# Order of the expert weight requests in the later pairs, and the place of VectorE's update of H

## The reference

```
for i in range(DEPTH):                       # 4 layers
    y = mixer_i(h)
    h = layer_norm(DN_ALPHA * h + y, ...)
    m = grouped_moe(h, ...)                  # for each of 16 experts e, with its gates:
                                             #   hidden = silu(t @ w1[e]) * (t @ w3[e]);  out += gate * (hidden @ w2[e])
    h = layer_norm(DN_ALPHA * h + m, ...)
```

## Time and profile before

| | us |
|---|---|
| median of three runs (lowest, highest) | 1929.92 (1926.3, 1935.45) |
| time of the profiled execution | 1932.07 |
| its span, first to last instruction | 1930.3 |
| TensorE busy | 1756.9 (91%) |
| VectorE busy | 683.1 (35%) |
| ScalarE busy | 456.9 (24%) |
| GpSimd busy | 149.1 (8%) |
| mean granted TensorE clock, as a share | 0.957 |
| DMA, mean over the span | 261 GB/s, 504.47 MB |

### The profile page before, as it was taken

One profiled execution on the slowest core, in us unless ns is written; L12 is line 12 of the kernel. 1 busy time (PEld: TensorE's weight loads), 2 busy tenths in 40 slices (PEclk: granted clock), 3 DMA queues, 4 the chain that ended last, 5 costly groups with the idle time before them and its releaser, 6 DMA issues. The chain is left out here.

```text
span 1930.3 us, 24276 instructions
## 1 busy us (share of the span) xinstructions
PE 1756.9 (91%) x8962; PEld 894.9 (46%) x8963; DVE 683.1 (35%) x1391; ACT 456.9 (24%) x894; POOL 149.1 (8%) x113
## 2 busy tenths in 40 slices
PE   8998979989897899899899988897989988899987
PEld 7867643333574443333244544332348757433332
DVE  3444462222425542222312226221243444532223
ACT  2664211111214111111111101111123834111111
POOL 1024100000300100000020100000030131100000
PEclk9999989999998899999999998898999999899999
DMA  9521168999932557679964236699993320579995
GB/s 336 188 95 46 50 273 359 428 428 423 338 131 87 196 231 311 243 304 429 406 248 168 109 158 283 261 410 395 427 357 131 131 88 2 196 299 427 428 428 204
DMA packets 84085, 504.47 MB, mean 261 GB/s; under 512 B 8259, under 2 KB 16500, under 8 KB 59132
## 3 DMA queue, kind: packets, MB, share of 16 engines
q1 hardware_dynamic: 72944, 488.65, 63.2%
q10 hardware_dynamic: 11020, 14.07, 2.2%
HBM read 501.64 MB, written 1.06 MB: 260 GB/s over the span
## 5 line engine op out<-in xcount | busy, mean ns | idle before, releaser
L1989 PE MATMUL bank<-ring,work 128*64 128x512 f32 x2176 | 476.9, 595 | 15.1 <-issue 10.4
L1989 PEld LDWEIGHTS bank<-ring,work 128*64 128x64 f32 x2176 | 156.4, 138 | 327.7 <-issue 319.0
L1507 DVE TENSOR_TENSOR work<-bank,work 64x512 f32<-64x512 f32 x64 | 67.9, 1062 | 539.2 <-ACT work L952 539.1
L1653 PE MATMUL bank<-HT,ring 128*128 128x256 f32 x1024 | 231.8, 387 | 0.0
L1653 PEld LDWEIGHTS bank<-HT,ring 128*128 128x128 f32 x1024 | 198.6, 194 | 37.2 <-issue 10.2
L1661 PE MATMUL bank<-ring,HT 128*128 128x512 f32 x448 | 197.4, 600 | 0.0
L2007 PE MATMUL bank<-w_slot,work 128*64 128x512 f32 x544 | 132.5, 632 | 18.6 <-DMA w_slot<-in_e_w 17.0
L952 ACT ACTIVATE work<-bank 64x512 f32<-64x512 f32 x64 | 37.7, 589 | 425.7 <-PE bank L1989 425.7
L1661 PEld LDWEIGHTS bank<-ring,HT 128*128 128x128 f32 x448 | 85.2, 193 | 103.6 <-issue 103.6
L2033 PE MATMUL bank<-work 128*128 128x512 f32 x256 | 121.4, 618 | 11.1 <-ACT work L977 6.0
L2007 PE MATMUL bank<-work 128*64 128x512 f32 x544 | 125.6, 604 | 5.6 <-DMA work<-in_e_w 4.0
(11 more groups left out here) (294 smaller groups left out, 1583.4 us busy)
## 6 DMA issues: line engine op xcount, KB each, us to landing
ring<-in_e_w SPq DMA_DIRECT2D x128, 2048.0 KB, 14.3
w_slot<-in_e_w SPq DMA_DIRECT2D x32, 2048.0 KB, 14.5
work<-in_e_w SPq DMA_DIRECT2D x32, 2048.0 KB, 16.5
ring<-in_a_w_in SPq DMA_DIRECT2D x15, 2048.0 KB, 20.1
ring<-in_c_w_in SPq DMA_DIRECT2D x8, 2048.0 KB, 23.8
ring<-in_b_w_in SPq DMA_DIRECT2D x6, 2048.0 KB, 24.6
ring<-in_a_w_out SPq DMA_DIRECT2D x4, 2048.0 KB, 8.5
ring<-in_c_w_out SPq DMA_DIRECT2D x4, 2048.0 KB, 7.7
```

The costliest lines, as they stand in the source:

```text
L1507: v.tensor_tensor(by_m(h_[j]), bank[b][CAP:, :], sil[j][CAP:, :], ALU.mult).then_inc(drained[b], 1)
L1653: ins = mm(dst[:, 0:SEQ], wt[:, k, n * P:(n + 1) * P], HT[:, k, :], start=k == 0, stop=k == KC - 1)
L1989: ins = mm(bank[b][lo:lo + CAP, :], x[:, k, :], wt[:, k, :], start=k == 0, stop=k == KC - 1, skip_group_check=True)
```

## The change

Two things are changed. First, `refill` is no longer a hardware loop but is written out seven times, and for p = 3 to 6 it asks in another order: behind step 1 the tiles q = 2, 3 of pair p + 1 as before, then, behind steps 3 and 4, the two down weights of pair p + 1, and only then the tiles q = 0, 1 of pair p + 2. Since step 4 is then past, these two are asked for right behind the down weight of half 1. For p = 0 to 2 the order stays. Second, VectorE's update of H becomes a function and is called in pair 0 behind the product of half 0, and with it the check for an extra pass of expert 0.

```diff
-                    def refill(p, d, more):
+                    def refill(p, d, more, down_first):
                         freed(i, p, 1)
                         for q in (2, 3):
                             load_up((n + 4 * (d + 1) + q) % SLOTS, i, p + 1, q)
-                        if more:
-                            freed(i, p, 2)
-                            for q in (0, 1):
-                                load_up((n + 4 * (d + 2) + q) % SLOTS, i, p + 2, q)
-                        for j in range(2):
-                            freed(i, p, 3 + j)
-                            load_down(i, p + 1, j)
-
-                    with sp.Fori(0, 2) as it:
-                        for d in range(3):
-                            refill(it * 3 + d, d, True)
-                    refill(6, 6, False)
+                        for part in (1, 0) if down_first else (0, 1):
+                            if part:
+                                for j in range(2):
+                                    freed(i, p, 3 + j)
+                                    load_down(i, p + 1, j)
+                            elif more:
+                                freed(i, p, 2)
+                                for q in (0, 1):
+                                    load_up((n + 4 * (d + 2) + q) % SLOTS, i, p + 2, q)
+
+                    for p in range(E // 2 - 1):
+                        refill(p, p, p < E // 2 - 2, p >= 3)
...
-                dve.wait_ge(spread_set, i + 1)
-                dve.wait_ge(rows_scaled, 2 * i + 1)
-                for tt in range(TT):
-                    own.then(v.tensor_tensor(H[:, tt, :].rearrange("t (p k) -> t k p", k=KC), XH[:, tt, :].rearrange("t (k p) -> t k p", k=KC),
-                                             gB[:, :].rearrange("t (p k) -> t k p", k=KC), ALU.mult))
-                own.wait()
-                for tt in range(TT):
-                    v.tensor_tensor(H[:, tt, :], H[:, tt, :], bB[:, :], ALU.add).then_inc(h_ready, 1)
+                def update_h():
+                    dve.wait_ge(spread_set, i + 1)
+                    dve.wait_ge(rows_scaled, 2 * i + 1)
+                    for tt in range(TT):
+                        own.then(v.tensor_tensor(H[:, tt, :].rearrange("t (p k) -> t k p", k=KC), XH[:, tt, :].rearrange("t (k p) -> t k p", k=KC),
+                                                 gB[:, :].rearrange("t (p k) -> t k p", k=KC), ALU.mult))
+                    own.wait()
+                    for tt in range(TT):
+                        v.tensor_tensor(H[:, tt, :], H[:, tt, :], bB[:, :], ALU.add).then_inc(h_ready, 1)
...
                     for j in range(2):
                         b = 2 + j
-                        with dve.If(counted[j] > CAP):
-                            over_sel(it, j, 1)
+                        if not (lead and j == 0):
+                            with dve.If(counted[j] > CAP):
+                                over_sel(it, j, 1)
                         dve.wait_ge(silu_h, it * 2 + (E * i + j + 1))
                         v.tensor_tensor(by_m(h_[j]), bank[b][CAP:, :], sil[j][CAP:, :], ALU.mult).then_inc(drained[b], 1)
+                        if lead and j == 0:
+                            update_h()
+                            with dve.If(counted[j] > CAP):
+                                over_sel(it, j, 1)
```

## The result

The changed kernel took 1937.84 us (median of 20 runs, 1928.39 to 1950.84), the kernel before 1931.44 (20 runs, 1924.78 to 1939.12). The ratio is 1.0035, with a 95% interval of 1.0019 to 1.0052: 3.7 to 10.0 us slower. Its profiled execution took 1936.12 us, with a span of 1934.3 where before had 1930.3.

What follows compares the result with a forecast made beforehand. The weight stream was taken to bound the later part of each expert stage. Order +5.5, clock +5.1 and VectorE -4.6 summed to +6.0 us, forecasting 1935.9, rounded 1936, with an 8-in-10 range of 1925 to 1945.

Steps and rivals of the forecast that it cites:

- order with clock: New request order in all four expert stages, +5.5 us, plus slower TensorE clock, about +5; 10.6 us forecast.
- VectorE: Pair 0 of each stage: the first product no longer stands behind the update of H; gain 4 x 1.16 = 4.6 us.
- the clock: TensorE drops to 1.2 GHz after the last wait, pair 7, in three of four stages; +5.1 us, bounds 0 and 6.8.
- Loads land in the order of the requests: Weight stream in the expert stages: loads land as asked, one each 4.89 us when the stream is full.
- rival (a): Only VectorE's part counts; queue places matter to nobody or loads don't land as asked: -4.6 us, 1925.3; chance 0.12.
- Stages 0 and 3: Full stream: waits move from down to up products, and the order gains 0.85 us in each stage, 1.7 together.
- 12 us of waits: TensorE's weight waits in a stage like 0 or 3, claimed not to go but to change places.
- Rival (b): Down weights first frees TensorE of 17.0 + 4.0 us of waits and slow groups: -32 us, 1897.5; chance 0.05.
- Rival (c): Queue runs dry in stages 0 and 3 as well, at the first changed refill: +20.2 us, 1950.1; chance 0.13.
- Stage 1: Half 0's down weight of pair 4 is asked of an empty queue; the whole stream runs late, loss 4.5 us.
- Stage 2: Queue is empty until half 1's down weight of pair 4 is requested at 1318.25, after TensorE's stop; loss 2.7 us.
- the stop would stay: TensorE's 9.88 us standstill at its loop's turn in stage 2 should remain, since the change leaves that loop alone.

Runs made afterwards that it cites:

- down_all: Against the kernel before: down weights asked for first behind every pair from the first on, loop written out, VectorE's update at its old place; 1962.82 us, ratio 1.0158.
- unroll_only: Against the kernel before: SyncE's loop written out with the old order of requests, VectorE's update at its old place; 1929.06 us, ratio 0.9998.
- order_only: Against the kernel before: SyncE's new written-out requests in the new order, VectorE's update of H at its old place; 1944.86 us, ratio 1.0064.
- fill_b: Changed kernel plus five matmuls in pair 7 ahead of the wait for half 1's weights; 1928.81 us, ratio 0.9991 to the kernel before.

## Why the prediction was right

**The sum.** +6.0 us were forecast, +6.8 (3.7 to 10.0) measured, within 0.5%. The parts, run alone, bear the terms out: order with clock 10.6 forecast and 12.4 measured, VectorE -4.6 and -2.3, both forecasts inside their intervals. The mechanism of the loss, a request that comes after the queue is empty, is shown. That the sum came within 1 us of the measured time is in part luck, since errors of 1 to 2 us in the terms went both ways: the clock took 3.1 us in the profile where 5.1 was forecast, the hole of stage 2 took 4.0 where 2.7 was, and a shorter stop, which the sum doesn't have, gave 1.5.

**Loads land in the order of the requests.** This held, and rival (a) falls: swapping requests moved the waits from the down to the up products. By the Trainium skill ("DMA: Bandwidth & Descriptors", section "Queues, rings and completion order") completion need not be in the order of issue; here the late request of 845.89 delayed the whole stream behind it (half 1 of pair 7 starts 4.6 us later), so for whole 2 MB loads of one engine the rule changed nothing.

**Stages 0 and 3.** The waits changed places, with 2.2 to 2.8 us in the middle of a pair where 2.9 was forecast. Their sum hardly changed: in stage 3 TensorE waited 9.6 us for weights before and 9.3 after. The prediction's "12 us of waits" is too much for such a stage; the rows add up to it only with the slow groups. Forecast were -0.85 for the order and -1.16 for VectorE, with +1.7 where the clock fell, which in the changed profile it did in stage 0 and not in stage 3: -0.3 and -2.0, measured +0.5 and -2.8. Rival (b) falls: down weights without waits freed nothing. Rival (c) falls for the changed kernel: in stage 3 the stream goes on at 428 GB/s from 1796 to 1826 us, across the request at 1801.22. down_all shows its mechanism, a queue that runs dry in stages 0 and 3 too; there they are 7.5 and 8.2 us longer.

**Stage 1.** The order alone was forecast at 4.5 us, and from pair 4 to half 1 of pair 7 it took 4.6. The down weight landed 8.0 us after its request, forecast 7.7, and that of half 1 after 9.4, forecast 10.2. The whole stage was forecast at 4.5 - 1.16 and up to 1.7 for the clock, so +3.3 to +5.0, and measured +5.9, with 1.4 of clock in the last half. The excess stands ahead of pair 4, in groups that ran in part at 1.2 GHz: the two slowest take 6.39 and 5.09 us in place of 5.35 and 5.08 in the kernel before, where 3.65 to 3.70 is full speed.

**Stage 2.** The hole came at the place forecast, 2.7 - 1.16 = +1.5 was forecast for the stage, and -0.2 measured. Two errors cancel in that. From pair 4 on the order took 4.0 us and not 2.7: the request of half 1 came at 1318.39 and landed 7.7 us later, as forecast, but the sixteen loads behind it took about 5.0 us each and not 4.89. Ahead of pair 4 the stage was 4.3 us shorter: VectorE's part, a stop that was 1.5 us shorter (8.42 for 9.88), and fewer slow groups. The kernel before was the odd one there: unroll_only, with the same order, has a stage 2 of 247.75. That the stop would stay was right, since the change leaves TensorE's code alone.

**The clock.** Three of four last up products were forecast slow. In the three profiles with the new order in every stage from p = 3 or earlier, it was two (after), four (order_only) and two (down_all). In the changed kernel they cost 1.7 and 1.4 us, 3.1 in place of 5.1. What it costs by itself was not timed: fill_b took it away, but the stop with it.

**VectorE.** The wait of pair 0 is gone in all four stages, and pair 1 starts 1.39 us sooner after pair 0 (35.51 for 36.90 in stage 1), where 1.16 was forecast: the idle time that the timeline prints was a little less than the delay. VectorE's dates came out as forecast: the first product starts 7.75 us after the stage's first up product, forecast 7.74. From its update on VectorE works without a gap up to the first compaction copy at 1708.96, 16.35 us after that start; before it was 17.68, and TensorE's gather, which it follows, came 1.38 us sooner. So the copy is at most 0.05 us late.

## What to carry to other kernels

When a stream of transfers is full, changing the order of the requests moves the waits and gains next to nothing; what can be lost is a request that comes after the queue is empty, and that is paid for some pairs later, where the stream bounds. To see such a loss, measure from the first changed request on: over a whole stage, a stop and a clock that had nothing to do with the change hid 4 us here. So put a transfer "in order of need" only where its trigger comes some microseconds before the queue ahead of it has landed (8.5 us, worked out from the kernel before for stage 3, were enough here, 2.7 were not), and keep the early triggers as filler elsewhere. Idle time that has no releaser and sits at a loop's turn deserves a count of the instruction fetches before the schedule is touched.

## What the runs showed of the hardware

In the kernels with 84 instruction fetches in all, TensorE's loop of stage 2 ran without a stop; in those with 93 it stood 8.4 to 10.5 us at the turn, and ten fetches in place of one stand in its second round. Some twenty more instructions in each of the two stages ahead of the loop (ten matmuls and ten weight loads each, by the profile's count) decided it. The Trainium skill ("Runtime: NRT & Kernel Launch", section "Instruction fetch mechanics") has the kind of stall, a taken branch to code outside the window; the trace agrees for stage 2's loop, with its ten fetches. Why the loops of stages 0, 1 and 3, with the same body, never showed a stop, and how the added code takes it away, stays open.

The second: a load that was asked for 2.7 us before the load ahead of it landed still landed 1.7 us later than in a full stream (6.6 for 4.89 us). In stage 3, with 8.5 us in hand by the rows of the kernel before, the stream went on at 428 GB/s.
